# Score and value products on 128 rows, with zeros in the rows that do not count, in a two-block f32 forward pass

## The reference

```python
def memory_attention(q, mem_k, mem_v):          # 4 heads of 64, layers 0 and 1 of the first block
    logits = einsum("bshd,bmhd->bhsm", qh, kh) * (HEAD_DIM ** -0.5)
    p = softmax(logits, axis=-1)
    o = einsum("bhsm,bmhd->bshd", p, vh)

def forgetting_attention(q, k, v, cum_logf):    # 12 heads of 64, layer 1
    logits = einsum("bqhd,bkhd->bhqk", qb, kb) * scale
    logits = logits + cum_logf[:, :, q0:kend, None] - cum_logf[:, :, None, :kend]
    p = softmax(where(kpos <= qpos, logits, -inf))
    outs.append(einsum("bhqk,bkhd->bqhd", p, vb))

def nsa_query_block(...):                       # 16 heads of 128 in 4 groups, second block
    o_c = einsum('bgrqn,bgnd->bgrqd', p_c, v_cmp)   # 15 compressed positions
    return gates[..., 0:1] * o_c + gates[..., 1:2] * o_s + gates[..., 2:3] * o_w
```

## Time and profile before

| | us |
|---|---|
| median of 3 runs | 1308.85 (1308.8 to 1309.37) |
| the profiled execution | 1308.61 |
| its span, first to last instruction | 1306.7 |
| PE busy with products | 1248.3 (96%) |
| VectorE busy | 890.6 (68%) |
| ScalarE busy | 639.6 (49%) |
| chain that ended last | PE 80%, VectorE 10%, issue 5%, ScalarE 4% |
| mean granted TensorE clock | 0.984 of full speed |

### The profile page before, as it was taken

How to read it: one execution, slowest core, us unless ns; L and a number is a source line. 1 busy time by engine, 2 the same in 40 slices (tenths; PEclk the granted TensorE clock), 3 DMA queues, 4 the chain that set the end, 5 groups by cost and what they waited for, 6 DMA issues and landing times.

```text
span 1306.7 us, 19500 instructions
## 1 busy us (share of the span) xinstructions
PE 1248.3 (96%) x8068; PEld 1113.8 (85%) x8068; DVE 890.6 (68%) x1358; ACT 639.6 (49%) x1015; POOL 12.4 (1%) x28
## 2 busy tenths in 40 slices
PE   6979999999999999999999999989899999999996
PEld 6956898999998868899999988767798989999885
DVE  5976578877765556788778856655476646666664
ACT  6544545555554334555546334425444545555453
POOL 0000000000000000000000000000000000000000
PEclk9989999999989999999999999999899899999999
DMA  9510344555442223355454543543455622222341
GB/s 389 225 65 1 123 144 153 215 204 178 177 162 97 98 97 117 142 209 203 178 186 161 196 173 147 192 154 132 159 194 185 233 106 98 97 98 97 119 176 60
DMA packets 28568, 200.54 MB, mean 153 GB/s; under 512 B 3393, under 2 KB 3521, under 8 KB 4929
## 3 DMA queue, kind: packets, MB, share of 16 engines
q1 hardware_dynamic: 28480, 199.30, 41.7%
HBM read 198.24 MB, written 1.05 MB: 153 GB/s over the span
## 4 chain that ended last, share of the span: by engine, by line
PE 80%; DVE 10%; issue 5%; ACT 4%; DMA 0%; DVEq 0%; POOL 0%; POOLq 0%; ACTq 0%; SPq 0%
PE bank L710 22%; PE bank L711 21%; PE bank L712 21%; DVE WL L1594 3%; PE bank L858 3%; ACT WH L1216 2%; DVE work L1776 2%; PE bank L1190 1%; PE bank L1165 1%; PE bank L922 1%; PE bank L1156 1%; PE bank L1173 1%; PE bank L1188 1%; DVE work L1729 1%; PE bank L844 1%
## 5 line engine op out<-in xcount | busy, mean ns | idle before, releaser
L1594 DVE TENSOR_TENSOR WL<-RAW,WH 128x2048 fp32r<-128x2048 f32 x180 | 411.8, 2291 | 175.1 <-ACT WH L1216 174.3
L1216 ACT ACTIVATE WH<-RAW 128x2048 fp32r<-128x2048 f32 x180 | 343.5, 1912 | 224.3 <-PE bank L712 220.7
L710 PE MATMUL bank<-XH,WH 128*128 128x256 f32 x1264 | 361.5, 286 | 18.2 <-DVE WL L1796 11.9
L711 PE MATMUL bank<-XL,WH 128*128 128x256 f32 x1264 | 358.1, 283 | 0.0
L712 PE MATMUL bank<-XH,WL 128*128 128x256 f32 x1264 | 358.0, 283 | 0.0
L710 PEld LDWEIGHTS bank<-XH,WH 128*128 128x128 f32 x1264 | 242.9, 192 | 22.6 <-DVE XL L1789 11.9
L711 PEld LDWEIGHTS bank<-XL,WH 128*128 128x128 f32 x1264 | 243.0, 192 | 0.5
L712 PEld LDWEIGHTS bank<-XH,WL 128*128 128x128 f32 x1264 | 242.9, 192 | 0.0
L710 PE MATMUL bank<-WH,MH 128*128 128x512 f32 (+1 forms) x544 | 202.5, 372 | 10.6 <-DVE work L2034 4.0
L711 PE MATMUL bank<-WL,MH 128*128 128x512 f32 (+1 forms) x544 | 199.8, 367 | 0.0
L712 PE MATMUL bank<-WH,ML 128*128 128x512 f32 (+1 forms) x544 | 199.4, 367 | 0.0
(11 more groups left out here) (256 smaller groups left out, 1593.1 us busy)
## 6 DMA issues: line engine op xcount, KB each, us to landing
RAW<-wstream SPq DMA_DIRECT2D x181, 1024.0 KB, 4.8
con<-consts SPq DMA_DIRECT2D x1, 1681.0 KB, 13.1
work<-xT_in SPq DMA_DIRECT2D x1, 1024.0 KB, 4.9
x<-x_in SPq DMA_DIRECT2D x1, 1024.0 KB, 10.7
work<-mem_in SPq DMA_DIRECT2D x1, 1024.0 KB, 15.9
xn<-memT_in SPq DMA_DIRECT2D x1, 1024.0 KB, 11.6
out_dram<-xn SPq DMA_DIRECT2D x2, 512.0 KB, 2.7
par<-params SPq DMA_DIRECT2D x1, 858.0 KB, 13.9
```

Source lines behind the costliest of these rows:

```text
L710: mm(o, ah, bh, start=start, stop=False)
L711: mm(o, ah, bl, start=False, stop=False)
L1216: act_fn(WH[:, t % RING, :], RAW[:, t % RING, :], ACT.Copy).then_inc(w_rounded, 1)
L1594: tt(WL[:, t % RING, :], RAW[:, t % RING, :], WH[:, t % RING, :].bitcast(F32), ALU.subtract).then_inc(w_split, 1)
```

## The change

Queries are stored twice, as two tiles. In tile e only the 64 rows of the heads with h % 2 = e hold queries; the other 64 rows hold zeros. The zeros come from the scaling itself: the factor is now a column of a small tile `hmask` that holds 64 ** -0.5 on one half of the partitions and 0 on the other. GpSimd fills it at the start. The score product then takes all 128 rows of query and key tile. For the compressed values, the tiles `vcm` and `ptC` are filled with zeros once, ahead of the heads, and the product takes all 128 rows of both.

```diff
-        q_mem = wk(0, 2, T)
-        q1 = wk(512, NMB, T)
+        q_mem = (wk(0, 2, T), wk(9952, 2, T))
+        q1 = (wk(512, NMB, T), wk(8416, NMB, T))
...
+            link(nc.gpsimd.memset(hmask[:, :], 0.0))
+            sync()
+            for e in range(2):
+                link(nc.gpsimd.memset(hmask[DH * e:DH * (e + 1), e:e + 1], DH ** -0.5))
+            sync()
+            pool.drain().then_inc(mask_made, 1)
...
-                        last = mm(o[:, i * T:(i + 1) * T], q_mem[r, h // 2, i * P:(i + 1) * P], mkt[r, l, h // 2, :],
+                        last = mm(o[:, i * T:(i + 1) * T], q_mem[h % 2][:, h // 2, i * P:(i + 1) * P], mkt[:, l, h // 2, :],
...
-                    mm(o[:, a:a + n], q1[r, h // 2, t], k1[r, h // 2, 0:n], start=True, stop=False)
+                    mm(o[:, a:a + n], q1[h % 2][:, h // 2, t], k1[:, h // 2, 0:n], start=True, stop=False)
...
-                    mm(o[:, 0:T], vcm[0:CMP_S, g, :], ptC[0:CMP_S, :], start=True, stop=False)
+                    mm(o[:, 0:T], vcm[:, g, :], ptC, start=True, stop=False)
...
+            def by_head(key, dst):
+                ready(dve, key)
+                src = B(key)[:, :].rearrange("p (b t) -> p b t", b=2)
+                for e in range(2):
+                    ins = stt(dst[e], src, hmask[:, e:e + 1], rbb, ALU.mult, ALU.mult)
+                free(ins, key, "dve")
...
-            scaled(("qm", 0), q_mem, DH ** -0.5)
+            dve.wait_ge(mask_made, 1)
+            by_head(("qm", 0), q_mem)
...
+            link(nc.vector.memset(vcm, 0.0))
+            link(nc.vector.memset(ptC, 0.0))
             dve.wait_ge(*act_a.next())
```

More of the change, by code:

```diff
@@ L381, in program @@
         stat = sb("stat", [P, 80])
-        WORK = 10400
+        hmask = sb("hmask", [P, 2])
+        WORK = 10464
         work = sb("work", [P, WORK])
@@ L496, in program @@
         prepared = sem("prepared")
+        mask_made = sem("mask_made")
         pool_const = sem("pool_const")
@@ L906, in score @@
                 kind, h = unit[0], unit[-1]
-                r = slice(DH * (h % 2), DH * (h % 2) + DH)
                 if kind == "mem":
@@ L1702, in attention @@
                         elif name == "q1":
-                            scaled((name, j), q1[:, 2 * j:2 * j + 2, :], DH ** -0.5)
+                            by_head((name, j), [q[:, 2 * j:2 * j + 2, :] for q in q1])
                         elif name == "qm":
-                            scaled((name, j), q_mem, DH ** -0.5)
+                            by_head((name, j), q_mem)
             def low_signal():
@@ L1903, in _ @@
             upto(("q1", 0))
-            scaled(("q1", 0), q1[:, 0:2, :], DH ** -0.5)
+            by_head(("q1", 0), [q[:, 0:2, :] for q in q1])
             upto(("v1", 0))
```

## The result

The changed kernel takes 1300.96 us (1299.94 to 1301.87, 4 runs) against 1308.89 us before: ratio 0.9938, 95% interval 0.9921 to 0.9956. The forecast was 1295.5 with a range of 1292.5 to 1299.0. The sign was right. Of the 13.3 us that were to go, 7.9 went, and the measured time lies outside the range.

A forecast was written before the change was run, and what follows sets the result against it. PE was taken to bound the two later stretches, a loop of waits the first. The terms 6.1 + 1.2 + 6.4 + 0.2 - 0.6 = 13.3 us came off the time, giving 1295.5 us, range 1292.5 to 1299.

The forecast's parts named there:

- The change between 64 or 16 and 128 rows is what costs: PE's score and compressed-value products: equal rows save 0.51 us per forgetting unit, 0.30 per second-memory unit, 0.40 per head.
- The rival by which half would go with the type and not with the rows: PE's steps: only half of each gain arrives, 1302.8 us; chance 0.10 together with the attentions left out.
- that of free rows: PE's gaps stay as they are and only VectorE's additions count, 0.6 us twice: 1310.0 us; chance 0.04.
- that by which nothing would go in the attentions since their values still write 64 rows: Both attentions gain nothing, only the compressed values do: 1303.7 us; chance 0.10 together with half the gain.
- The added VectorE work: Five more scalings of 690 ns: +0.60 us at 57.71, +0.60 at the output projection, others covered; mask operand and fills nothing.
- The first stage: First memory attention, 66 to 112 us: +0.60 for scaling, -0.8 from three score units at 0.27 each, net -0.2 us.
- The sum of the steps: Whole kernel: 6.1 + 1.2 + 6.4 + 0.2 - 0.6 = 13.3 us less.
- The forgetting unit: Forgetting attention's scores on PE: 1.65 us per unit becomes 1.14, 0.51 less; 12 units, 6.1 us.
- the second memory attention: Its score products on PE: 0.30 us less per unit, four units, 1.2 us.
- The failed step: Bound on TensorE's clock phase: low-level stretches may appear or go in later stages, 2 to 3 us either way.
- The clock rival: From 66 to 112 us a longer PE wait keeps the clock at 1.2 GHz, costing about 15 us: 1310.6 us; chance 0.02.

The follow-up runs named there:

- the scores alone: The changed kernel with the compressed values back on 16 rows and without the fills, scores still on 128 rows: 1306.80 us, ratio 0.9979 to the kernel before.

## Why the prediction was wrong, step by step

- *The change between 64 or 16 and 128 rows is what costs.* Right, and to the size: 1.10 for a unit where 1.14 was expected, 0.40 per head by the steps, 0.39 by the stretch. The rival by which half would go with the type and not with the rows falls with the same rows. So do that of free rows, and that by which nothing would go in the attentions since their values still write 64 rows. The load takes 184 ns with 64 rows and 191 with 128, next to the same; the price lies in a load that starts only with its product (447.37 and 447.37) instead of ahead of it (457.94 and 458.16). The Trainium skill (TensorE: Matmul & The Clock Gate, LDWEIGHTS (loading the stationary operand)) states that the time of a load follows its columns and not its rows. The trace agrees on the load itself, 184 against 191 ns, and not where the rule is read as one on the time of the whole product.
- *The added VectorE work.* Right in place: the chain after has L1672 twice for 1.32 us at 57.76 where it had 0.60, and PE's wait at the output projection is 1.90. The sizes were 0.12 and 0.11 low. A second instruction costs nearly its full length, which moreover is not 690 ns: the mask as a per-partition operand, which I put at nothing, makes each scaling 745 ns long. The fills took 0.48 and 0.27 us in the wait of 0.97 and cost nothing. The ten scalings (ns, min/median/max):

```profile
L1672 DVE SCALAR_TENSOR_TENSOR work<-bank,hmask,rb x10: 740/745/751, 57.7 to 460.4; 128x512 f32<-128x512 f32 x10
```

- *The first stage.* The scores gain 0.19 per round on the chain (0.88 for 1.07), not 0.27. The last taps of the stage start at 120.69 for 120.49 us, 0.2 later where 0.2 earlier was forecast; by the first forgetting score the two kernels are level.
- *The sum of the steps*: 13.3 forecast, 13.1 found in the profile. The forgetting unit and the second memory attention gained a little more than forecast; the scalings cost a little more, and the first stage gained nothing. That these nearly cancel is luck.
- *The failed step* is the bound, in the words of the prediction: "A stretch at the low level may appear or go: 6 us at half speed cost 3, so I allow 2 to 3 either way". It was 4.4 us in the profiled execution and 5.2 at the median (13.1 less 7.9), all to one side. I looked at the one stage whose clock was low, instead of listing every wait of PE of two microseconds or more. There were two such waits in the retention layer, of 4.03 and 2.19 us, and in the kernel before the first was followed by only 3.4 us at the low level and the second by none. Behind them the changed kernel has 6.7 and 3.4 us at the low level. I also lengthened a third wait, from 1.2 to 1.9 us, and priced only the wait; behind it stand another 3.4.
- *The clock rival* had the right mechanism in the wrong stage and the wrong size. It watched 66 to 112 us, where the clock stayed at 0.93 in the profiled execution, and got a chance of 0.02. Its sum was wrong too: 30 us of work at the high level take 60 at the low one and cost 30 more, not 15.

The chain rows of the changed kernel for the first stage, to be read against the earlier trace rows (the second column is us):

```profile
57.76 1.32 DVE work L1672 x2
...
77.61 0.61 DVE stat L1703
...
86.31 0.88 PE bank L921 x4
```

Open: what decides, wait by wait, whether the clock falls. The same wait of 1.9 us at the output projection was followed by the low level in the changed kernel and not in the scores alone. Two executions of the changed kernel differ in the first attention (0.93 and 0.89), and so do kernels that differ only behind it.

## What to carry to other kernels

Here a product on 64 rows between products on 128 cost some 0.27 us more than one on 128 (0.55 in a unit of two), and one on 16 rows 0.40, its neighbours' share included. Zeros that fill the rows cost nothing on PE. That pays where PE is the bound and another engine has time to write the zeros. When a change takes time out of PE's stream, list every wait of PE behind it with its granted clock, before forecasting that the gain arrives. A wait of 2 to 4 us may be worth filling with products that nobody reads; in both kernels here it was.

## What the runs showed of the hardware

- A weight load of 128 rows behind a product on 64 rows started with its own product, at 447.37 us both; behind one on 128 rows it started 0.22 us ahead (457.94 and 458.16).
- A factor taken from a column of a tile instead of a number made VectorE's scaling of 128x512 745 ns long instead of 690.
- Thirty filler products of 0.23 us each, in waits of 1.9, 4.0 and 2.2 us (1.2 for the first in the kernel before), took 8 us off the changed kernel and 3.6 off the kernel before.
- 1.15 us of added work cost 4.0 us at the median. A lower mean clock goes with the rest (0.980 in six of eight executions); that it came of moving the waits is likely and not shown.
- The changed kernel's executions on one chip lay at 1299.9 and 1300.1, or at 1301.8 and 1301.9, with mean clocks of 0.979 and 0.978. One more stretch of 3.4 us at the lower level would account for the 1.7 us; only one of the four was profiled.
- Rows of short products also came before a low level: 48 products of 12 columns (near 383 us, 6.8 or 10.2 us of it), 48 of 48 columns (near 1015 us, 6.8). That they are the cause is not shown. Weaving them into a wide projection gave no clear answer: of the three profiled executions with it, the first place had a clock of 1.00 in one, 3.4 us at the low level in another and 10.2 us in the third, and the second place 3.4 us in each instead of 6.8.
